# Scaling attention probabilities inside the transposing product: a diagonal of reciprocals in place of the identity

## The reference

```python
s = jnp.einsum('bnqkgd,bnskd->bnkgqs', qb, kb).astype(F32) * ATTN_SCALE   # 8 blocks of 128 queries x 256 keys, 8 heads
p = sink_softmax(s, mask, sink)      # exp(s - m) / (sum exp(s - m) + exp(sink - m))
o = jnp.einsum('bnkgqs,bnskd->bnqkgd', p.astype(vb.dtype), vb)
```

## Time and profile before

| What | Value |
| --- | --- |
| Time, median of 3 runs | 3167.29 us (3165.85 to 3167.81) |
| Time of the profiled execution | 3167.29 us |
| Its span, first to last instruction | 3165.3 us |
| TensorE matmul busy | 91% of the span |
| VectorE / ScalarE / GpSimd busy | 46% / 26% / 19% |
| Mean granted TensorE clock | 0.945 |
| Chain that ended last, by engine | TensorE 77%, VectorE 15%, ScalarE 4% |
| Attention stage of the first layer | about 301 to 396 us from the span's start |
| Attention stage of the second layer | about 1861 to 1956 us |

### The profile page before, as it was taken

The page is one execution under the profiler, slowest core; times in us unless marked ns, Lnnn a source line. Parts: engine busy times, 40 slices in busy tenths (PEclk is TensorE's granted clock), DMA queues, the critical chain, the costliest instruction groups (busy, mean ns, idle before and its releaser), DMA issues.

```text
span 3165.3 us, 49209 instructions
## 1 busy us (share of the span) xinstructions
PE 2885.1 (91%) x20858; PEld 2722.5 (86%) x20858; DVE 1453.9 (46%) x2517; ACT 830.3 (26%) x1739; POOL 613.3 (19%) x295
## 2 busy tenths in 40 slices
PE   6997766999899999999999967689998999999997
PEld 6996635878899999999999956368798999999997
DVE  5334749775622222222363265697855222223224
ACT  3111642442411111111321035524333111111112
POOL 2320001023321222212123200100341222221123
PEclk9998966999999999999999988679999999999998
DMA  3112000023211111111221020000331111111111
GB/s 123 47 34 67 1 27 7 19 93 102 70 47 41 43 52 47 47 47 47 70 73 47 21 67 1 28 8 28 119 96 47 48 52 43 47 47 47 41 54 54
DMA packets 55881, 158.12 MB, mean 50 GB/s; under 512 B 9200, under 2 KB 23536, under 8 KB 54896
## 3 DMA queue, kind: packets, MB, share of 16 engines
q1 hardware_dynamic: 52496, 150.76, 15.1%
q0 software_dynamic: 3168, 4.23, 0.5%
HBM read 137.43 MB, written 17.54 MB: 49 GB/s over the span
## 4 chain that ended last, share of the span: by engine, by line
PE 77%; DVE 15%; ACT 4%; issue 3%; DMA 1%; SPq 0%; DVEq 0%; POOL 0%; ACTq 0%
PE bank L1606 21%; PE bank L1608 21%; PE bank L1607 21%; PE bank L1976 1%; PE bank L1972 1%; DVE a_stats L1097 1%; PE bank L1867 1%; PE bank L1952 1%; PE bank L1962 1%; PE bank L1833 1%; PE bank L1775 1%; DVE n_square_sum L1443 1%; DVE act_low L1455 1%; DVE c_T L1222 1%; DVE c_NT L1220 1%
## 5 line engine op out<-in xcount | busy, mean ns | idle before, releaser
L1606 PE MATMUL bank<-act_high,w_high 128*128 128x344 f32 x3504 | 1134.7, 324 | 42.5 <-POOL w_low L493 24.3
L1608 PE MATMUL bank<-act_high,w_low 128*128 128x344 f32 x3504 | 1126.2, 321 | 0.0
L1607 PE MATMUL bank<-act_low,w_high 128*128 128x344 f32 x3504 | 1125.8, 321 | 0.0
L493 POOL TENSOR_TENSOR w_low<-w_raw,w_high 128x1024 fp32r<-128x1024 f32 x206 | 529.6, 2577 | 1670.0 <-ACT w_high L583 1665.8
L1606 PEld LDWEIGHTS bank<-act_high,w_high 128*128 128x128 f32 x3504 | 665.5, 190 | 48.1 <-POOL w_low L493 24.8
L1607 PEld LDWEIGHTS bank<-act_low,w_high 128*128 128x128 f32 x3504 | 664.3, 190 | 2.5 <-issue 1.9
L1608 PEld LDWEIGHTS bank<-act_high,w_low 128*128 128x128 f32 x3504 | 665.2, 190 | 0.0
L1465 DVE TENSOR_TENSOR f_mid<-f_silu,bank 128x344 f32<-128x344 f32 x132 | 67.7, 513 | 851.3 <-PE bank L1608 851.3
L1566 DVE TENSOR_TENSOR resid<-bank,resid 128x344 f32<-128x344 f32 x528 | 270.4, 516 | 209.8 <-PE bank L1608 209.8
L583 ACT CAST w_high<-w_raw 128x1024 fp32r<-128x1024 f32 x206 | 213.1, 1045 | 504.6 <-PE bank L1608 500.4
L1606 PE MATMUL bank<-f_mid_high,w_high 128*128 128x344 f32 x1056 | 341.3, 323 | 4.1 <-DVE resid L1566 4.0
(11 more groups left out here) (287 smaller groups left out, 2942.1 us busy)
## 6 DMA issues: line engine op xcount, KB each, us to landing
w_raw<-wts SPq DMA_DIRECT2D x206, 512.0 KB, 3.7
resid<-x SPq DMA_DIRECT2D x4, 1376.0 KB, 10.2
att_keep<-act_low SPq DMA_DIRECT2D x2, 2064.0 KB, 6.6
act_low<-att_keep POOLq DMA_DIRECT2D x6, 688.0 KB, 6.0
x_keep<-resid SPq DMA_DIRECT2D x3, 1376.0 KB, 6.3
o_y<-resid SPq DMA_DIRECT2D x3, 1376.0 KB, 5.7
resid<-x SPq DMA_DIRECT2D x4, 516.0 KB, 7.7
resid<-x_keep SPq DMA_DIRECT2D x4, 516.0 KB, 6.6
```

Source lines behind the costliest of these rows:

```text
L493: eng.tensor_tensor(wl[s][:, :], raw[s][:, :], wh[s][:, :].bitcast(F32), ALU.subtract).then_inc(w_low, 1)
L1606: mm(out, wh[s][:, wcols], act_h, start=start, stop=False)
L1607: mm(out, wh[s][:, wcols], act_l, start=False, stop=False)
L1608: return mm(out, wl[s][:, wcols], act_h, start=False, stop=stop)
```

## The change

The probabilities are no longer scaled in place. VectorE writes, for each block, a tile of 128 x (8 x 128) that holds for each head the identity times the reciprocal of the row sum ("diag"), and TensorE multiplies each 128x128 tile of unscaled exponentials by its head's diagonal. That is now a plain float32 product and not a transpose instruction; it transposes and scales at once. ScalarE loses its three scaling operations and takes over the copy "ptc2" from VectorE. Two diagonal tiles alternate; they lie where the rotary key tables lay before the stage. TensorE's wait for the two "p_last" becomes one for "diag".

```diff
+        dg = [at(f"a_diag_recip{q}", 8 * 128, RING + 5088 + 1024 * q)[:, :].rearrange("p (h t) -> p h t", h=8) for q in range(2)]
...
 # ScalarE
                     if V:
+                        eng.wait_ge(tensor_val, at_block("tensor_val", "pt2", l, n - 1))
+                        eng.copy(pT[:, 8:12, :], bank[4][:, :].rearrange("p (h t) -> p h t", h=4)).then_inc(scalar_val, val.step("ptc2"))
                         eng.wait_ge(tensor_val, at_block("tensor_val", "pt3", l, n - 1))
...
-                    if M:
-                        eng.wait_ge(vector_soft, at_block("vector_soft", "recip", l, n))
-                        for h in range(5, 8):
-                            a(sm[q][:, h, :], sm[q][:, h, :], ACT.Copy, scale=st(6, h, 1)).then_inc(scalar_soft, soft.step("p_last" if h == 7 else None))
...
 # VectorE
-                            if b == 0 and V:
-                                eng.wait_ge(tensor_val, at_block("tensor_val", "pt2", l, n - 1))
-                                eng.tensor_copy(pT[:, 8:12, :], bank[4][:, :].rearrange("p (h t) -> p h t", h=4)).then_inc(vector_val, val.step("ptc2"))
-                    if V and not S:
-                        eng.wait_ge(tensor_val, at_block("tensor_val", "pt2", l, n - 1))
-                        eng.tensor_copy(pT[:, 8:12, :], bank[4][:, :].rearrange("p (h t) -> p h t", h=4)).then_inc(vector_val, val.step("ptc2"))
...
+                        if n > 1:
+                            eng.wait_ge(tensor_val, at_block("tensor_val", "pt3", l, n - 2))
                         eng.wait_ge(vector_soft, at_block("vector_soft", "recip", l, n))
-                        for h in range(5):
-                            ts(sm[q][:, h, :], sm[q][:, h, :], rd[:, h:h + 1], None, ALU.mult).then_inc(vector_soft, soft.step("p_last" if h == 4 else None))
+                        tt(dg[q], bcast(ident, 1, 8), bcast(rd, 2, 128), ALU.mult).then_inc(vector_soft, soft.step("diag"))
...
 # TensorE
                         for k in range(4):
                             h, kt = (4 * w + k) // 2, k % 2
-                            last = mm(bank[4 + w % 2][:, 128 * k:128 * k + 128], sm[o][:, h, 128 * kt:128 * kt + 128], ident,
-                                      is_transpose=True, start=True, stop=True)
+                            last = mm(bank[4 + w % 2][:, 128 * k:128 * k + 128], sm[o][:, h, 128 * kt:128 * kt + 128], dg[o][:, h, :],
+                                      start=True, stop=True)
...
-                        eng.wait_ge(vector_soft, at_block("vector_soft", "p_last", l, n - 1))
-                        eng.wait_ge(scalar_soft, at_block("scalar_soft", "p_last", l, n - 1))
+                        eng.wait_ge(vector_soft, at_block("vector_soft", "diag", l, n - 1))
```

More of the change, by code:

```diff
@@ L1669, in probs_t @@
                         if w == 0:
-                            eng.wait_ge(vector_val, at_block("vector_val", "ptc2", l, n - 2))
+                            eng.wait_ge(scalar_val, at_block("scalar_val", "ptc2", l, n - 2))
                         elif w == 1:
@@ L1709, in blocks @@
                         eng.wait_ge(scalar_val, at_block("scalar_val", "vp", l, n - 1))
-                        eng.wait_ge(vector_val, at_block("vector_val", "ptc2", l, n - 1))
+                        eng.wait_ge(scalar_val, at_block("scalar_val", "ptc2", l, n - 1))
                         eng.wait_ge(scalar_val, at_block("scalar_val", "ptc3", l, n - 1))
```

## The result

| | before | after |
| --- | --- | --- |
| Time, median of 7 runs | 3167.05 us (3165.85 to 3168.64) | 3178.11 us (3174.06 to 3189.01) |
| Ratio | | 1.0040, 95% interval 1.0030 to 1.0049 |
| Profiled execution: time, span | 3167.29, 3165.3 us | 3174.06, 3170.7 us |

Slower, as forecast. But the profiled execution is the fastest of the seven, at +6.8 us just where the forecast of 3174.1 lies (+5.4 of it in the span, +1.4 outside it); the median is 4 us above it, the ratio puts the kernel 12.7 us behind, and the changed kernel's runs are spread over 15 us where those before lay within 3. The two slowest (3186.62 and 3189.01 us) have a mean granted clock of 0.943, the other five, the median among them, 0.945 or 0.946. So there are two things to explain: the stage, and the spread.

What follows compares the result with a forecast made beforehand. The prediction took a chain of waits, mostly VectorE with TensorE's pt2 and pt3, to bound the attention stages. Its terms made +3.4 us a layer, +6.8 on 3167.3, so 3174.1 us; own range 3171.5 to 3176.5, overall 3168 to 3179.

Steps and rivals of the forecast that it cites:

- what bounds the stage: Attention stages: a round's chain runs almost wholly on VectorE, with one excursion to TensorE's pt2 and pt3.
- the sign: Whole kernel: slower, +6.8 us (+0.21%); chances 0.57 slower, 0.33 same, 0.10 faster.
- den: VectorE, each round: starts 2.68 us after the first score operation instead of 3.00, so -0.32 us, not -0.60.
- The terms in the stage: Attention, per layer: call 1 +1.7, six rounds of +0.40, call 8 +0.9, call 7 -1.6, together 3.4 us.
- the products: TensorE's pt2 and pt3, each round: 1.99 us in place of 1.09, +0.90 us on the chain.
- TensorE's round without waits: TensorE in the attention stage: 9.6 us, under the forecast round of about 10.3, so it doesn't become the bound.
- Rival 1: Call 7: the clock falls all the same, adding 2 x 5.0 us, 3177.3 us; chance 0.13.
- the gain of 1.6 us: Call 7, each layer: the shorter TensorE wait keeps the clock up, -1.6 us.
- Rivals 3, 4 and 5: Product costs one transpose (3160.9 us, 0.08); product costs four transposes (3215 us, 0.03); diagonal at half pace (3190 us, 0.05).
- Rival 2: VectorE sheds all of ptc2, or the clock gives back a little later: 3.4 us less, 3170.7 us; chance 0.16.
- The step that failed: Sample tokens' attention behind the stage: shifted clock changes taken as 0, allowing 1 us a layer either way.

Runs made afterwards that it cites:

- The products alone: Kernel before, with pt0 to pt3 as plain float32 products with the identity and the scaling as before: 3182.13 us, ratio 1.0056.
- look 1: Another traced execution of the changed kernel, nothing altered: 3174.91 us.
- look 4: Another traced execution of the changed kernel, nothing altered: 3176.38 us.
- look 2: Another traced execution of the changed kernel, nothing altered: 3185.95 us.
- look 3: Another traced execution of the changed kernel, nothing altered: 3197.10 us.
- the last experiment: Changed kernel with the output's low part moved behind the next call's ptc0, plus one unread 1.2 us row maximum per layer: 3175.57 us, ratio 1.0021.
- the pure delay: Kernel before, with four unread row maxima on VectorE at the end of the stage in each layer: 3182.64 us, ratio 1.0050.
- the late low part on the changed kernel: Changed kernel with the low part of a block's attention output moved behind the next call's ptc0: 3188.21 us, ratio 1.0058.
- the copy alone: Kernel before, with only the copy ptc2 moved from VectorE to ScalarE: 3172.99 us, ratio 1.0017.
- the transposes back: Changed kernel with identity transposes instead of diagonal products, diagonal still written, probabilities unscaled, for timing only: 3168.81 us, ratio 1.0007.

## Why the prediction was right and wrong

*Right: what bounds the stage and the sign.* The chain ran where it was put, TensorE didn't become the bound, ScalarE came up at den, and pt2 and pt3 carried the cost. The products alone cost +0.96 a round.

*The terms in the stage.* Between the seven row maxima of calls 0 to 6 the stage grew by 1.53 us (into call 1) and 5 x 0.55; the diagonal took 0.18 off ahead of them, the calls behind added 0.30: together 4.4. The forecast's were 1.38, 5 x 0.40, -0.18 and +0.2: together 3.4. Mis-sized were the products (2.05 us, not 1.99: record follows record at 0.112 us, but the first step behind a wait takes 0.213, which pv's 32 records had averaged away), the step from reciprocal to diagonal (0.31 us for 0.24, taken as unchanged), and den (-0.30, not -0.32). That makes 0.15 a round, and 2 us in the kernel. TensorE's round without waits is 9.84 us and not 9.6; it was close to the bound, but not over it. Rival 1 (the clock falls in call 7) didn't come in any of the five traces: the gain of 1.6 us was real, behind a wait of 1.66 us. Rivals 3, 4 and 5 fell: a product costs two records of 0.112 us each, and the diagonal 1.23 us. Rival 2 came in one half: den waited, but the rests of the layers gave 3.0 us back in the first trace and 2.9 in look 1 (0.1 in look 4). The factor of four that the Trainium skill (TensorE: Matmul & The Clock Gate, section Terms) gives for float32 didn't appear: it would have made a round of over 13 us.

*The step that failed* is the last: "a shift moves where these changes fall; I take 0 and allow 1 us a layer either way". The rests of the two layers moved by -1.3 and -1.7 us in the first trace, -1.1 and -1.8 in look 1, +1.9 and -2.0 in look 4, and by +8.1 to +9.7 in the three layers with a late rise (looks 2 and 3). That the fastest execution meets the forecast is luck, from errors that cancel: +9.6 in the two attention parts for 6.8, -3.0 in the rests, -1.2 in the start, which belongs to no edit, so +5.4 in the span, and +1.4 outside it. The ratio contains executions with a late rise: the two slowest of the seven have the granted clock that goes with one (0.943, and 0.942 in look 2). The median has not: its granted clock is 0.946. That it lies 4 us over the forecast comes to 2 us from the mis-sized stage; the rest is scatter among the good executions (3174.06 to 3181.21 us), whose source stays open. I had read the clock's changes at the place of the edit only, not in the stretches behind it, where before already had long stretches of half clock.

*What the late rise depends on.* The products and ScalarE's copy are not enough for it: both are in the last experiment, whose eleven runs lie within 5 us. Whether it comes without them isn't settled: the products alone and the pure delay have runs some 9 us above their others with a lower granted clock, but all five traced late rises are in kernels with both. Not on a longer stage: the late low part on the changed kernel made the stage shorter and the late rises more frequent (four of five runs by their granted clock), and one operation of 1.2 us took them away again. What is left is the moment at which the stage ends, against the falls of the clock: the sorting by 1.70 to 2.04 us fits every trace, but it is an association and not an experiment. Why the clock then holds at half 150 us later was not found, nor whether an edit at the sample tokens' products or in the chunk loop can make the kernel robust.

*Where the gain went.* The change took 0.60 us of copy and 0.18 of scaling off VectorE's round. Of the 0.60 only 0.30 arrived: ScalarE's own chain from pt3 to sinkexp was just behind, and VectorE now waits 0.21 us for it. What it paid with was TensorE's time, on the one stretch in which VectorE waits for TensorE.

## What to carry to other kernels

Work moved to an engine with slack still costs if it lands on the one stretch in which the others wait for it: here TensorE was idle for 1.9 us a round, and the 0.96 fell where it wasn't. Look instead for what sits on the chain and could run in its gap: moving one 0.60 us operation behind the copy that TensorE waits for gained 6 us, with no work saved. And where a kernel has long stretches of half clock behind the edit, take several executions before believing one trace: here a shift of a tenth of a microsecond (1.59 against 1.70) went with 10 us more or less.

## What the runs showed of the hardware

The granted clock can stay at half while TensorE is busy in every microsecond: in look 3 it is at half from 547.1 to 581.2 us, and by its windows TensorE is busy for 23.70 of the 23.7 us from 557.5 on. TensorE had come back to work at 554.9, so 26 us almost without a gap passed before the rise; in the first trace of the changed kernel it was 7 us (550.5 to 557.4). In both, the low stretch had begun ahead of that work.

```profile
557.50:581.20 23.70, 23.70 (x235) 21.04 (x236) 14.33 (x28) 6.61 (x19) 0.00 (x0) 0.50 0.01 1
```

And waits of 1.71 us (the copy alone) and 1.61 to 1.70 us (the transposes back) in each round, with transposes on either side, went with a fall of the clock in one round of one layer of each trace, while in the traces of the kernel before waits of 1.36 and 0.52 us in the rounds never did.

A float32 product of 128x128 by 128 columns takes two matmul records: the 16 of pt0 and pt1 in the changed kernel follow each other at 0.112 us, the 8 of the transposes at 0.109 us. Behind a wait the first step is longer, 0.213 us for the products of pt2 and 0.166 for the transposes. And a tensor-tensor operation of VectorE over 128x1024 whose operands are read with steps of zero took 1.23 us, with the next start after 1.14: as with plain operands (1.22 and 1.14).
